# The first attention of a one-core transformer kernel rebuilt around its projections; the split activations taken straight from the transposes' bank; first products by contraction block

## Time and profile before

| what | value |
|---|---|
| runs | 1249.76, 1252.72, 1258.08 us |
| profiled execution | 1247.78 us, span 1245.7 us |
| TensorE matmul busy | 1155.2 us, 93% |
| POOL busy | 827.4 us, 66% |
| ACT busy | 582.8 us, 47% |
| VectorE busy | 559.4 us, 45% |
| mean transfer rate | 191 GB/s |
| first projections to the end of the first attention | 38.1 to 160.2 us |
| layer 0 output product | 163.4 to 188.0 us |
| network of layer 0, of layer 1, of the second block | from 196.2, 534.4, 1051.5 us |

### The profile page before, as it was taken

How to read it: one execution, slowest core, us unless ns; L and a number is a source line. 1 busy time by engine, 2 the same in 40 slices (tenths; PEclk the granted TensorE clock), 3 DMA queues, 4 the chain that set the end, 5 groups by cost and what they waited for, 6 DMA issues and landing times.

```text
span 1245.7 us, 21662 instructions
## 1 busy us (share of the span) xinstructions
PE 1155.2 (93%) x8119; PEld 1043.1 (84%) x8119; DVE 559.4 (45%) x1149; ACT 582.8 (47%) x868; POOL 827.4 (66%) x290
## 2 busy tenths in 40 slices
PE   6899798999999876999999989999999998999996
PEld 2799687999996873989999959999998987999995
DVE  4359666766557886375322372224211234111113
ACT  0443525554542435354554515455777543554452
POOL 3567448988882730689888825656565765988884
PEclk9899989999998988999999998999999998999998
DMA  9788567999984350678655523444444553666661
GB/s 342 262 292 231 187 209 233 345 335 320 301 301 151 98 136 1 220 227 263 202 179 175 170 65 93 144 135 137 136 139 136 187 165 103 194 192 183 188 185 67
DMA packets 253193, 237.69 MB, mean 191 GB/s; under 512 B 18043, under 2 KB 216496, under 8 KB 253136
## 3 DMA queue, kind: packets, MB, share of 16 engines
q1 hardware_dynamic: 237312, 202.80, 52.6%
q10 hardware_dynamic: 14784, 31.98, 7.1%
q0 software_dynamic: 1040, 2.12, 0.5%
HBM read 235.83 MB, written 1.05 MB: 190 GB/s over the span
## 4 chain that ended last, share of the span: by engine, by line
PE 72%; DVE 8%; ACT 7%; POOL 5%; DMA 5%; issue 2%; SPq 0%; DVEq 0%; POOLq 0%; ACTq 0%
PE bank L1147 18%; PE bank L1148 18%; PE bank L1149 18%; POOL unit_lo L688 5%; ACT unit_hi L790 3%; DMA raw<-in_ev_w_in 2%; PE bank L1186 2%; PE bank L1172 2%; PE bank L1174 2%; PE bank L1218 2%; PE bank L1206 1%; DMA att<-in_ada_w 1%; PE bank L1208 1%; PE bank L1226 1%; PE bank L1327 1%
## 5 line engine op out<-in xcount | busy, mean ns | idle before, releaser
L688 POOL TENSOR_TENSOR unit_lo<-raw,unit_hi 128x2048 fp32r<-128x2048 f32 (+4 forms) x88 | 349.3, 3973 | 261.0 <-ACT unit_hi L790 260.9
L1147 PE MATMUL bank<-h_hi,unit_hi 128*128 128x256 f32 x1248 | 354.2, 284 | 0.3
L1148 PE MATMUL bank<-h_lo,unit_hi 128*128 128x256 f32 x1248 | 353.5, 283 | 0.0
L1149 PE MATMUL bank<-h_hi,unit_lo 128*128 128x256 f32 x1248 | 353.4, 283 | 0.0
L722 POOL TENSOR_TENSOR unit_lo<-raw,unit_hi 128x2048 fp32r<-128x2048 f32 (+1 forms) x70 | 257.2, 3675 | 70.5 <-ACT unit_hi L922 66.9
L1147 PEld LDWEIGHTS bank<-h_hi,unit_hi 128*128 128x128 f32 x1248 | 239.6, 192 | 5.0 <-issue 1.3
L1148 PEld LDWEIGHTS bank<-h_lo,unit_hi 128*128 128x128 f32 x1248 | 239.6, 192 | 2.7
L1149 PEld LDWEIGHTS bank<-h_hi,unit_lo 128*128 128x128 f32 x1248 | 239.6, 192 | 0.0
L790 ACT ACTIVATE unit_hi<-raw 128x2048 fp32r<-128x2048 f32 (+4 forms) x98 | 163.2, 1666 | 105.9 <-PE bank L1149 38.0
L725 POOL TENSOR_TENSOR down<-raw_down,down 128x1024 fp32r<-128x1024 f32 x70 | 176.2, 2517 | 0.0
L1862 DVE SCALAR_TENSOR_TENSOR work<-bank,cols,work 128x254 f32<-128x254 f32 (+1 forms) x176 | 72.7, 474 | 146.9 <-ACT work L909 146.9
(11 more groups left out here) (310 smaller groups left out, 2065.1 us busy)
## 6 DMA issues: line engine op xcount, KB each, us to landing
raw<-in_ffn_w_up SPq DMA_DIRECT2D x88, 512.0 KB, 5.2
raw<-in_w_in SPq DMA_DIRECT2D x60, 512.0 KB, 4.6
raw_down<-in_ffn_w_down SPq DMA_DIRECT2D x44, 512.0 KB, 4.9
raw<-in_w_up SPq DMA_DIRECT2D x64, 256.0 KB, 3.1
raw_down<-in_w_down SPq DMA_DIRECT2D x32, 512.0 KB, 3.5
raw<-in_ev_w_in SPq DMA_DIRECT2D x28, 512.0 KB, 5.3
ada<-in_ada_w ACTq DMA_DIRECT2D x13, 1024.0 KB, 7.8
att<-in_ada_w SPq DMA_DIRECT2D x12, 1024.0 KB, 7.7
```

The costliest lines, as they stand in the source:

```text
L688: nc.gpsimd.tensor_tensor(ul[g % 2][:, w], raw[g % 2][:, w], uh[g % 2][:, w].bitcast(F32), ALU.subtract).then_inc(lo_up, 1)
L1147: nc.tensor.matmul(o, sh, mh, start=first, stop=False)
L1148: nc.tensor.matmul(o, sh, ml, start=False, stop=False)
L1149: return nc.tensor.matmul(o, sl, mh, start=False, stop=last)
```

## The change

Four edits come together.

1. **The first attention.** The four CX units are no longer multiplied before the attention: CX and BG together, 12 halves, are its fill in the pattern of FOX and MOBA. On VectorE, the convolutions move into the attention (`dsa_middle`, `dsa_between`), as does the multiplication by the gate; ACT's copies for them move with them (`even_filler`). All outputs of the pairs go to bank 6, since the sums use bank 7; `out_low` of the pair before then comes first in a pair's turn, and `out_high` right after the copies of the transposed weights. One q unit is put ahead of the indexer; the others follow it.
2. **The loads.** The modulation sums are spread anew: 4 and 5, then 6 and 7 ahead of the indexer, 8 after its head 3, 9 to 12 in the attention after each pair, 13 to 15 after the first three residual blocks. SP loads the pieces up to 10 between units. Pieces 11 to 15 are started by ACT, each after a wait for an earlier sum. The table of constants moves from POOL's queue to SP's, the gate rows from POOL's to ACT's.
3. **High halves from the bank.** For n = 1 to 5, ACT scales and shifts straight from PSUM into hh, one block kt at a time, each counted; VectorE makes all of hf; POOL subtracts for banks 0 to 2 and VectorE for bank 3. For a given bank the two engines take turns.
4. **First units by contraction block.** The first unit (n = 4 and 5: the first two) is multiplied block by block: for each kt, all products with hh, of high and of low weights; then those with hl. The unit after it (`second_unit`) does all products with high weights ahead of those with low ones. For n = 0 the low weights stay last. `keep_warm` before n = 2 goes from 8 to 5.

```diff
-                turn(("pv", a, h // 2), 6 + h // 2 % 2)
+                turn(("pv", a, h // 2), 6 if a == DSA else 6 + h // 2 % 2)
...
-        FILL = {DSA: [[(G_BG[0], 0), (G_BG[0], 1)], [(G_BG[1], 0)], [(G_BG[1], 1)], [], [], [], [], []],
+        FILL = {DSA: halves(G_CX + G_BG, (3, 1, 2, 1, 2, 1, 1, 1)),
...
-        SUM_IDX = {0: [6], 2: [7], 4: [8], 6: [9]}
-        SUM_CONV = [10, 11]
-        SUM_EVEN = [12, 13, 14, 15]
+        SUM_EARLY = [6, 7]
+        SUM_IDX = 8
+        SUM_ATT = [9, 10, 11, 12]
+        SUM_EVEN = [13, 14, 15]
...
+            early = {G_KI: SUM_EARLY[0], G_QKV[DSA][0]: SUM_EARLY[1], G_QKV[DSA][2]: SUM_IDX, G_QKV[DSA][3]: SUM_ATT[0],
+                     G_QKV[DSA][4]: SUM_ATT[1]}
+            for g in range(G_KI, G_EO[-1] + 1):
                 load_unit(g)
+                if g in early:
+                    load_ada(early[g])
...
+                for q in range(3):
+                    evacuated(pool, ("ht", n, q))
+                    pool.wait_ge(h_hi, highs(n, 2 * q + 1))
                     k = slice(2 * q, 2 * q + 2)
                     nc.gpsimd.tensor_tensor(hl[:, k, :], hf[:, k, :], hh[:, k, :].bitcast(F32), ALU.subtract
-                                            ).then_inc(h_lo[0], 1)
+                                            ).then_inc(h_lo_pool, 1)
...
+                for q in range(4):
                     o = full(act, ("ht", n, q))
+                    if q % 2:
+                        evacuated(act, ("ht", n, q))
                     for i in range(2):
                         kt = 2 * q + i
-                        dst, src = hf[:, kt, :], o[:, S * i:S * (i + 1)]
+                        dst, src = hh[:, kt, :], o[:, S * i:S * (i + 1)]
...
+                        ins.then_inc(h_hi, 1)
...
+            def load_sum(a):
+
+                act.wait_ge(ada_acc, a - 1)
+                act.dma_start(ada[a % 2].rearrange("p (t n) -> p t n", t=KD // 2), ada_half(a)).then_inc(ada_in[a % 2], 16)
+
+            AHEAD = {2: SUM_ATT[2], 3: SUM_ATT[3], 5: SUM_EVEN[0]}
+
+            def even_filler(g):
+
+                (cg if g < G_BG[0] else gated)(g)
+                if g == G_CX[1]:
+                    for w in range(2):
+                        load_gates(act, 0, w)
+                if g - G_CX[0] in AHEAD:
+                    load_sum(AHEAD[g - G_CX[0]])
...
+            def first_units(n, gs, rows=False, low_last=False):
...
+                for kt in range(KD):
+                    pe.wait_ge(h_hi, highs(n, kt))
+                    for part in parts:
+                        multiply(part, kt, uh, hh, start=kt == 0 and part[3] == 0)
+                        if not low_last:
+                            multiply(part, kt, ul, hh)
+                for g in gs:
+                    for kt in range(KD):
+                        h_low_ready(n, kt)
+                        for part in parts:
+                            if part[0] != g:
+                                continue
+                            last = kt == KD - 1 and not low_last
+                            mm = multiply(part, kt, uh, hl, stop=last and ends(part))
...
-            keep_warm(8)
+            keep_warm(5)
...
                 for p in range(PAIRS):
+                    if p and a == DSA:
+                        out_low(a, p - 1)
                     for h in (2 * p + 2, 2 * p + 3) if p + 1 < PAIRS else ():
                         normalize(a, h)
+                    if middle:
+                        middle(p)
                     for h in (2 * p + 4, 2 * p + 5) if p + 2 < PAIRS else ():
                         soft(a, h)
-                    if p:
+                    if p and a != DSA:
                         out_low(a, p - 1)
                     if between:
                         between(p)
...
+            def dsa_middle(p):
+
+                if p < 3:
+                    convolution((0, 2, 3)[p])
 
             def dsa_between(p):
+
+                if p == 0:
+                    convolution(1)
+                if p >= 2:
+                    gate(p - 2)
+                modulation_half(SUM_ATT[p], bank[7][:, :])
```

More of the change, by code:

```diff
@@ L975, in _ @@
             nc.scalar.activation(wi, b[:, 0:16], ACT.Copy).then_inc(free("wi"), 1)
+            evac_qkv(G_QKV[DSA][0], 0, 0)
             for h in range(HEADS):
@@ L1178, in unit_cols @@
                     if i == 0:
-                        for kt in range(nkt if high else 0):
-                            pe.wait_ge(*ready(kt))
-                            a = slice(slot(g) + kt * n + c, slot(g) + kt * n + c + P)
-                            nc.tensor.matmul(o[:, 0:S], uh[s][:, a], ml[:, kt, :], start=False, stop=False)
                         pe.wait_ge(lo_up, g + 1)
@@ L1188, in unit_cols, with unit_rows @@
                     mm.then_inc(bank_full[4 + s], 1)
-            def unit_rows(g, sth, stl, ready=None, order=None, part=None, high=None):
+            def unit_rows(g, sth, stl, ready=None, order=None, part=None):
                 o = bank[4 + g % 2] if part else unit_begin(g)
@@ L1211, in unit_rows @@
                     if tt == 0:
-                        for kt in order if high else ():
-                            pe.wait_ge(*ready(kt))
-                            nc.tensor.matmul(c, stl[:, kt, t], uh[s][:, slot(g) + kt * n:slot(g) + kt * n + n],
-                                             start=False, stop=False)
                         pe.wait_ge(lo_up, g + 1)
@@ L1221, in unit_rows, with second_unit @@
                     mm.then_inc(bank_full[4 + s], 1)
+            def second_unit(g, rows=False):
+                o, s, w = unit_begin(g), g % 2, units[g].get("n", UC)
+                for weight in (uh, ul):
+                    if weight is ul:
+                        pe.wait_ge(lo_up, g + 1)
+                    for i in range(2):
+                        c = o[:, w * i:w * (i + 1)] if rows else o[:, S * i:S * (i + 1)]
+                        for kt in range(KD):
+                            a = slot(g) + kt * w
+                            for h in (hh, hl) if weight is uh else (hh,):
+                                first, last = kt == 0 and i == 0 and h is hh and weight is uh, weight is ul and kt == KD - 1
+                                if rows:
+                                    mm = nc.tensor.matmul(c, h[:, kt, P * i:P * (i + 1)], weight[s][:, a:a + w], start=first, stop=last and i == 1)
+                                else:
+                                    mm = nc.tensor.matmul(c, weight[s][:, a + P * i:a + P * (i + 1)], h[:, kt, :], start=first, stop=last and i == 1)
+                mm.then_inc(bank_full[4 + s], 1)
             def keep_warm(n):
@@ L1430, in _ @@
             mod_columns(0, (0,), first=False, js=[4, 5, 6, 7, 12, 13, 14, 15])
-            for g in G_QI:
-                unit_cols(g, hh, hl, ready=h_ready(0), high=h_high_ready(0))
+            first_units(0, G_QI[:1], low_last=True)
+            unit_cols(G_QI[1], hh, hl)
             unit_cols(G_KI, hh, hl, blocks=(64, 0))
+            unit_cols(G_QKV[DSA][0], hh, hl)
             pe.wait_ge(wi_rows, 1)
@@ L1480, in _ @@
             mod_columns(1, (0,))
-            keep_warm(8)
+            keep_warm(5)
             transpose_rows(2, x, 3)
-            for g in G_Z:
-                unit_rows(g, hh, hl, ready=h_ready(2), high=h_high_ready(2))
+            first_units(2, G_Z[:1], rows=True)
+            second_unit(G_Z[1], rows=True)
+            for g in G_Z[2:]:
+                unit_rows(g, hh, hl)
             mod_rows(1, 0)
@@ L1549, in _ @@
             transpose_rows(4, xn, 9)
-            unit_cols(G_F, hh, hl, blocks=(0,), ready=h_ready(4), high=h_high_ready(4))
+            first_units(4, [G_F, G_QKV[FOX][0]])
+            second_unit(G_QKV[FOX][1])
             for j, g in enumerate(G_QKV[FOX]):
+                if j < 2:
+                    continue
                 if j < 4:
```

225 lines of the change are left out of this document (121 added, 104 removed).

## The result

| kernel | median of runs (us) | ratio to before, 95% interval | profiled execution, span (us) |
|---|---|---|---|
| before | 1253.87 (1249.76 to 1258.08) | | 1247.78, 1245.7 |
| after | 1234.65 (1227.38 to 1235.01) | 0.9837 [0.9809, 0.9864] | 1234.9, 1233.1 |

The change makes the kernel 1.6% faster; 1231 was predicted. But the sum was made against the profiled execution, and there 12.6 us of span went, not 21.0. The rest of the 19 us between the medians is the place of the two profiled executions among their runs: that of before lay 6 us under its median, that of after at its own. So the time came out near the forecast partly by luck, and the steps have to be judged by the traces.

What follows compares the result with a forecast made beforehand. TensorE carries 72% of the chain, so time is won only where it waits. Gains of 10.7 + 3.0 + 7.3 = 21.0 us off the profiled 1247.8 give 1226.8; with the median 4.9 above, 1231 us, range 1217 to 1246.

Steps and rivals of the forecast that it cites:

- First attention: CX units and first attention: with 12 halves as fill, 59.2 us become 48.5, a gain of 10.7 us.
- Rival A: First attention bound by its order, not by fill; gain of 12 us in all, 1241 us; chance 0.15.
- Indexer: Indexer and its cover, from 59.7 to 101.0 us: TensorE's waits go, gain 3 us (bounds 0 and 3.5).
- The selection is hidden: Selection after the indexer: 17.9 us on VectorE, ending near 97 us before the scores at 97.6; cost 0.
- The output product is dense and only shifts: Output product after the first attention: 24.6 us busy of 24.6, so it only moves earlier.
- Network of layer 0: Start of layer 0's network: split activations and first units by block gain 2.2 us of 3.0 (bounds 0 and 3).
- Before Z: Ahead of the units Z: three fewer `keep_warm` products give 2.6 us, in all 2.7 (bounds 1.5 and 6).
- Network of layer 1: Start of layer 1's network: the same gain as at layer 0's, 2.2 us.
- Second block: Second block's start: G_F's evacuation moves about 1.5 us later, a term of -1 us (bounds -2 and 2).
- Last network: Last network, from edits 3 and 4: gain of 1.2 us (bounds 0 and 2).
- Rival B: Edits 3 and 4 give nothing, through POOL's longer turn or the clock at 0.5; 1239 us, chance 0.12.
- Rival C: First attention: fill and softmax do not overlap, 76.4 us against 59.2; slower, 1270 us; chance 0.04.

Runs made afterwards that it cites:

- e10: Kernel after with the table of constants and layer 0's gate rows back on GpSimd's queue, as before the change; 1235.52 us, ratio 0.9854.
- e3: Kernel after with the two norm rows (2 x 512 KB) started after the third EO unit, not ahead of the output product; 1229.65 us, ratio 0.9828.
- e4: Kernel after with pieces 11 to 15 of ada_w back on SP's queue, gate and norm rows staying with ACT; 1230.42 us, ratio 0.9826.
- e1: Kernel before with edits 1 and 2 alone (rebuilt first attention, loads on two queues); 1238.1 us, ratio 0.9902.
- e9: Kernel after, GpSimd's second low half ahead of its subtractions, in layer 0's and 1's networks only after VectorE normalized the rows; 1229.41 us, ratio 0.9800.
- e2: Kernel before with edits 3 and 4 alone (high halves from the bank, first units by block, keep_warm 5); 1250.51 us, ratio 0.9996.
- e5: Kernel after with GpSimd's second low half ahead of its subtractions, without waiting for the normalized rows; 1238.62 us, ratio 0.9880.

## Why the prediction was right or wrong

- **First attention, 10.7 us: right**, 61.6 to 50.9 (the product for the gate rows is in both). TensorE waits there for `out_low` (2.1 us) and for a convolution's bank (1.4), the two places named, 3.5 us where I had 1.7. Rival A's mechanism, an attention bound by its order, did not come.
- **Indexer, 3.0: 4.2.** What pays is the loads: e10 puts the placing of the constants and gate rows at 6 to 8 us in the projections. I had named that edit but priced it inside a term bounded by TensorE's idle time, as if a late load could cost no more than the idling of the kernel before.
- **The selection is hidden: right, closely.** It ended at 99.54, not 97, since it took 21.3 us instead of 17.9:

```profile
78.24 1.12 DVE L2084 TENSOR_TENSOR work<-work,consts 128x128 f32<-128x128 f32 x1
...
85.13 1.63 DVE L2089 TENSOR_SCALAR work<-work 128x128 f32<-128x128 f32 x1
...
95.46 3.61 DVE L2089 TENSOR_SCALAR work<-work 128x256 f32<-128x256 f32 x1
```

  Three instructions were held, each until GpSimd's low half ended (79.21, 86.68 and 98.92 us), and the two longest were not two-input adds but one-input ones, the last of which took 0.29 us in the kernel before. 2.8 us behind the scores, it cost nothing, by the 5 us of fill that I had counted as its cover.
- **"The output product is dense and only shifts": wrong, the step that failed.** It cost 7.4 us. I looked for an exposed load only at piece 15 and gave the second queue nothing. But 3 MB started on ACT's queue within 4.3 us, around the third unit's load, 1 MB of them rows that my sum never placed; e3 and e4 return 6 of the 7.4. The rule that said so stood in my rival A, but tied to the attention, where it did no harm, and not carried on to the stretch behind.
- **Network of layer 0, 2.2: -1.4.** The first unit ended 2.3 us earlier (3.0 worked out), then it was taken back: TensorE waited for the low half behind GpSimd's chain, and ACT for the load behind that. I had seen its third subtraction and charged 1 us; I had not followed the load that waits for the low half behind it. With timely loads (e4) the stage gives 0.1.
- **Before Z, 2.7: 1.3**, and e1, which has neither edit 3 nor edit 4, gains about 1 there as well. My 2.6 us for six halves of `keep_warm` do not come from the row that I showed: 9.97 us for 16 make 3.7 for six, more than the 2.9 by which the rows were ahead, and that row stands at a clock of 0.71 (e1's 16 took 7.11 at 1.00). I had not foreseen that the transposes would wait for the rows, 2.44 us, nor the lower clock behind it. The wait for the latent rows grew by 1.9. VectorE is held on its last steps to them while GpSimd works from 421.39 for 6.38 us, but it was held as long before. The kernel before, then the kernel after:

```profile
430.36 4.82 DVE L2052 TENSOR_SCALAR att<-accg,small 128x384 f32<-128x384 f32 x1 [1.47 <-POOL small L702]
```

```profile
421.45 4.67 DVE L2154 TENSOR_SCALAR att<-accg,small 128x384 f32<-128x384 f32 x1 [1.47 <-POOL small L698]
426.04 1.89 DVE L2155 TENSOR_SCALAR att<-accg,small 128x256 f32<-128x256 f32 x1
```

  What grew is the restoring ahead of it, 11.75 us to 12.89; the rest of the 1.9 stays open. With 8.46 in e9 the wait is 4.7 again.

- **Network of layer 1, 2.2: 0.6. Second block, -1: +1.1. Last network, 1.2: 3.4.** In the last one the units are half as long and the second low half was already ahead of the subtractions; that the edit pays in full there for these reasons was not tested. In the second block G_F's later evacuation did not show in the lead. In sum 5.0 of 7.3 came; e1 gains 0.8 after the output product without edits 3 and 4, so they gave 4.2, which agrees with e2's 4.4.
- The span: 15.0 us of lead at the output product's start (13.7 predicted), 7.4 lost in it, 5.0 gained after it: 12.6.
- **Rival B** (edits 3 and 4 give nothing) has its number in e2, where they stand alone (ratio 0.9996), but not its mechanism: e2 loses 4.2 us up to the end of the output product, 3.2 of them in the projections, and wins 4.4 behind it. Rival C (no overlap of fill and softmax) did not come.
- **The bounds.** The upper ends of the terms of edits 3 and 4 add to 16 us, not 14, and the low ends to -0.5, not 0. So the fastest end is 1216.5, just outside the stated range; it changes nothing here.

## What to carry to other kernels

A load that is moved to another queue is not moved away: list every transfer in flight around each unit's load, queue by queue, and price a collision by how long such a load took to land, not by the idle time of the kernel before. When a stage starts earlier, follow the buffer chain (low half, next load, next copy) two units on; the gain stays only if that chain moves too. Idle time of one engine is free to fill only if no other engine is held meanwhile: here GpSimd's free 4.7 us contained the 1.5 us in which VectorE normalized. And a wait has to be compared with the kernel before, instruction by instruction, before it is put down to a hold: the hold ahead of the latent rows was there all along.

## What the hardware showed that I had not expected

- One-input float32 `TENSOR_SCALAR` instructions of VectorE between SBUF tensors were held by GpSimd's subtractions: normalizing 5.65 us instead of 1.53 (e5), a 128x256 `TENSOR_SCALAR` 3.61 us where it took 0.29 in the kernel before. I had read the exclusion as one of two-input instructions only. `MAX8` and `MATCH_REPLACE8` in the same stretch kept their 0.29 and 0.28 us, and `TENSOR_SCALAR` out of PSUM ran beside the subtractions at its 0.5 us.
- Two queues moved near the same number of packets, not of bytes: from 146 to 161 us ACT's moved 1340 packets and SP's 1588, but ACT's carried 3.14 MB and SP's 1.58, 2.3 KB a packet against 1.0. ACT's took 60.9% of the engines' time and SP's 32.2%, while SP's half unit landed in 13.8 us against a median of 6.5 for this tensor. In e3 it was 862 packets with 1.73 MB against 1056 with 1.05. That larger packets in SP's own loads would mend this was not tested.
- The granted clock fell behind short waits: 0.62 and 0.53 behind 1.6 and 2.5 us of waiting in the output product, 0.50 behind the 2.44 us ahead of the transposes. The same identity products, 128x512, cost 0.62 us each at 0.71 (before), 0.44 at 1.00 (e1).
